# The order of VectorE's products in a head's preparation: near levels first, 256- and 512-token ones last

## The reference

```
S_t = diag(a_t) S_{t-1} + k_t v_t^T ;  o_t = S_t^T q_t
score(t, s) = sum_d q[t,d] k[s,d] exp(b[t,d] - b[s,d]),  s <= t,  b = cumsum(log a)
o_t = sum_s score(t, s) v_s
```

## Time and profile before

| | |
|---|---|
| median of 3 runs | 1294.83 us (1294.48 to 1295.87) |
| the profiled execution | 1293.82 us |
| its span in the trace | 1292.1 us |
| TensorE busy | 1235.5 us, 96% of the span |
| VectorE busy | 599.9 us, 46% |
| ScalarE busy | 415.4 us, 32% |
| GpSimd busy | 85.2 us, 7% |
| mean granted TensorE clock | 0.988 of 2.4 GHz |

### The profile page before, as it was taken

One profiled execution on the slowest core, in us unless ns is written; L12 is line 12 of the kernel. 1 busy time (PEld: TensorE's weight loads), 2 busy tenths in 40 slices (PEclk: granted clock), 3 DMA queues, 4 the chain that ended last, 5 costly groups with the idle time before them and its releaser, 6 DMA issues.

```text
span 1292.1 us, 15169 instructions
## 1 busy us (share of the span) xinstructions
PE 1235.5 (96%) x6099; PEld 1021.0 (79%) x6099; DVE 599.9 (46%) x714; ACT 415.4 (32%) x442; POOL 85.2 (7%) x121
## 2 busy tenths in 40 slices
PE   4699999999999999989999999999999999999996
PEld 3578888888889997867887788888988888888885
DVE  6855556456343667456645333335523233232221
ACT  4522322222222365343434322223422222222222
POOL 5100000000000032022310000000000000000000
PEclk9999999999999999988999999999999999999998
DMA  9276555555252422111221222243123332222311
GB/s 379 66 241 193 172 171 178 195 184 165 90 184 93 131 65 66 35 39 60 66 66 33 66 83 85 93 130 98 48 83 97 97 97 97 97 89 67 114 57 65
DMA packets 119789, 143.40 MB, mean 111 GB/s; under 512 B 3892, under 2 KB 102336, under 8 KB 119744
## 3 DMA queue, kind: packets, MB, share of 16 engines
q1 hardware_dynamic: 119560, 142.69, 33.6%
q10 hardware_dynamic: 184, 0.07, 0.0%
HBM read 140.65 MB, written 2.10 MB: 110 GB/s over the span
## 4 chain that ended last, share of the span: by engine, by line
issue 48%; PE 39%; DVE 6%; ACT 3%; DMA 2%; POOL 1%; SPq 0%; ACTq 0%; POOLq 0%; DVEq 0%
PE PS L478 10%; PE PS L480 10%; PE PS L479 10%; PE PS L682 3%; DVE ACC L1300 2%; PE PS L608 1%; ACT WH L873 1%; PE PS L521 1%; DMA RAW<-in_w_in_mix_dram 1%; PE PS L522 1%; PE PS L523 1%; DMA RAW<-in_ffn_w_in_dram 1%; DVE W L1440 1%; PE PS L722 1%; DVE WL L1200 0%
## 5 line engine op out<-in xcount | busy, mean ns | idle before, releaser
L478 PE MATMUL PS<-HH,WH 128*128 128x512 f32 (+1 forms) x1064 | 416.9, 392 | 7.4 <-DVE HL L1222 4.0
L479 PE MATMUL PS<-HL,WH 128*128 128x512 f32 (+1 forms) x1064 | 408.1, 384 | 0.0
L480 PE MATMUL PS<-HH,WL 128*128 128x512 f32 (+1 forms) x1064 | 408.0, 383 | 0.0
L1200 DVE TENSOR_TENSOR WL<-RAW,WH 128x2048 fp32r<-128x2048 f32 (+1 forms) x97 | 216.9, 2236 | 345.1 <-ACT WH L873 345.1
L873 ACT ACTIVATE WH<-RAW 128x2048 fp32r<-128x2048 f32 (+1 forms) x97 | 180.8, 1864 | 407.8 <-PE PS L480 370.6
L478 PEld LDWEIGHTS PS<-HH,WH 128*128 128x128 f32 x1064 | 201.2, 189 | 53.1 <-issue 6.8
L480 PEld LDWEIGHTS PS<-HH,WL 128*128 128x128 f32 x1064 | 201.1, 189 | 43.2
L479 PEld LDWEIGHTS PS<-HL,WH 128*128 128x128 f32 x1064 | 201.4, 189 | 41.3 <-issue 1.1
L478 PE MATMUL PS<-UH,WH 128*128 128x512 f32 (+1 forms) x372 | 140.2, 377 | 0.0
L479 PE MATMUL PS<-UL,WH 128*128 128x512 f32 (+1 forms) x372 | 139.8, 376 | 0.0
L480 PE MATMUL PS<-UH,WL 128*128 128x512 f32 (+1 forms) x372 | 139.6, 375 | 0.0
(11 more groups left out here) (225 smaller groups left out, 1187.6 us busy)
## 6 DMA issues: line engine op xcount, KB each, us to landing
RAW<-in_ffn_w_in_dram SPq DMA_DIRECT2D x44, 1024.0 KB, 5.2
ADAW<-in_w_ada_dram SPq DMA_DIRECT2D x56, 512.0 KB, 5.6
RAW<-in_w_in_mix_dram SPq DMA_DIRECT2D x22, 1024.0 KB, 5.2
RAW<-in_ffn_w_down_dram SPq DMA_DIRECT2D x16, 1024.0 KB, 5.2
ADA<-in_w_ada_dram SPq DMA_DIRECT2D x8, 1024.0 KB, 14.0
RAW<-in_ffn_w_down_dram SPq DMA_DIRECT2D x7, 768.0 KB, 4.8
RAW<-in_w_out_dram SPq DMA_DIRECT2D x3, 1024.0 KB, 5.1
XST<-in_x_dram SPq DMA_DIRECT2D x4, 512.0 KB, 5.1
```

Of the source, the lines that this page charges most:

```text
L478: mm(ps, whi, ahi, start=start, stop=False)
L479: mm(ps, whi, alo, start=False, stop=False)
L480: return mm(ps, wlo, ahi, start=False, stop=stop)
L1200: V.tensor_tensor(WL[s][:, 0:size], RAW[s][:, 0:size], WH[s][:, 0:size].bitcast(F32), ALU.subtract)\
```

## The change

The block of `decayed` that forms W256 and W512 moves behind the loop over the near levels; its instructions are the same. As the order of the 18 increments of `prep` is changed with it, TensorE's near batches now wait for 6, 10 and 14 of a preparation's increments (before: 10, 14 and 18), and the far scores for all 18 (before: 6).

```
-                pe.wait_ge(prep, 18 * p + 6 + 4 * (g + 1))
+                pe.wait_ge(prep, 18 * p + 2 + 4 * (g + 1))
...
-                pe.wait_ge(prep, 18 * p + 6)
+                pe.wait_ge(prep, 18 * p + 18)
...
                 V.tensor_tensor(KL[:, :], KL[:, :], k, ALU.mult).then_inc(prep, 1)
-                dve.wait_ge(exps, 10 * p + 3)
-                dve.wait_ge(prep, 18 * p + 2)
-                (W256: four products, W512: two products)
                 for l, B in enumerate(LEVELS):
                     h = B // 2
                     dve.wait_ge(exps, 10 * p + 4)
                     qp = QP[:, l, :].rearrange("p (n h) -> p n h", h=h)
                     V.tensor_tensor(qp, qp, blocks(q, B)[:, :, h:B], ALU.mult).then_inc(prep, 1)
                     dve.wait_ge(exps, 10 * p + 5 + l)
                     kp = blocks(KP[:, l, :], B)[:, :, 0:h]
                     V.tensor_tensor(kp, kp, blocks(k, B)[:, :, 0:h], ALU.mult).then_inc(prep, 1)
+                dve.wait_ge(exps, 10 * p + 3)
+                dve.wait_ge(prep, 18 * p + 2)
+                for src, c0 in ((KL, 0), (QU, 2)):
+                    for j in range(2):
+                        cs = slice(4 * j + c0, 4 * j + c0 + 2)
+                        ins = V.tensor_tensor(blocks(W256[:, :], CHUNK)[:, cs, :], blocks(src[:, :], CHUNK)[:, cs, :],
+                                              FT[:, 0, cs].unsqueeze(2).to_broadcast([P, 2, CHUNK]), ALU.mult)
+                    ins.then_inc(prep, 1)
+                for src, c0 in ((KL, 0), (QU, 4)):
+                    cs = slice(c0, c0 + 4)
+                    V.tensor_tensor(blocks(W512[:, :], CHUNK)[:, cs, :], blocks(src[:, :], CHUNK)[:, cs, :],
+                                    FT[:, 1, cs].unsqueeze(2).to_broadcast([P, 4, CHUNK]), ALU.mult).then_inc(prep, 1)
```

More of the change, by code:

```diff
@@ L1433, in decayed @@
                 V.tensor_tensor(KL[:, :], KL[:, :], k, ALU.mult).then_inc(prep, 1)
+                for l, B in enumerate(LEVELS):
+                    h = B // 2
+                    dve.wait_ge(exps, 10 * p + 4)
+                    qp = QP[:, l, :].rearrange("p (n h) -> p n h", h=h)
+                    V.tensor_tensor(qp, qp, blocks(q, B)[:, :, h:B], ALU.mult).then_inc(prep, 1)
+                    dve.wait_ge(exps, 10 * p + 5 + l)
+                    kp = blocks(KP[:, l, :], B)[:, :, 0:h]
+                    V.tensor_tensor(kp, kp, blocks(k, B)[:, :, 0:h], ALU.mult).then_inc(prep, 1)
                 dve.wait_ge(exps, 10 * p + 3)
@@ L1447, in decayed @@
                                     FT[:, 1, cs].unsqueeze(2).to_broadcast([P, 4, CHUNK]), ALU.mult).then_inc(prep, 1)
[L1448 to L1455, removed]
             diag = SC[:, :].rearrange("p (i x) -> p i x", x=5 * P)[:, :, 0:P]
```

## The result

The changed kernel takes 1282.3 us (median of 4 runs, 1280.62 to 1284.87) against 1295.35 us before (4 runs, 1294.48 to 1296.1). The ratio is 0.9906, 95% interval 0.9887 to 0.9925, so it is faster by 13 us. The forecast was 1280.5 with a range of 1278.7 to 1287.0. The profiled execution took 1284.87 us, the slowest of the four; its span is 1283.1 us.

The account below looks back on a forecast made before the run. TensorE, with work for 96% of the span, was taken as the bound. Waits 5.2 plus clock 9.7, less 0.1 and 0.5 of new waits, gave 14.3 us gained: 1280.5 us, range 1278.7 to 1287.0.

Parts of the forecast that it names:

- The waits: First near scores of heads 1 to 3: waits shrink to 1.04, 1.42 and 1.15 us, 5.2 us gained in sum.
- the plain price: Head 3: near products at 0.75 us beside GpSimd throughout, scores at 593.12; the forecast took 592.95, GpSimd finishing earlier.
- The clock: Low-clock stretches behind the waits of heads 1 to 3 mostly vanish: 9.7 us gained, ends 0 and 9.9.
- unit 10: Next weights in head 3: TensorE arrives before their split is ready, a new wait of 0.5 us.
- the first rival: Clock still falls in one or more heads, 1.7 to 3.3 us per fall: 1282.2 to 1287 us; 30%.
- the second one's milder form: Clock falls in all three heads, each low stretch half as long: 1284.8 us; 11% for the whole rival.
- the case that it was worked out for: Forecast case: shortened waits in heads 1 to 3 and clock mostly up there, 1280.5 us, spanning 1279 to 1282; 50%.
- stays up: Clock mostly at full behind the remaining waits of 1.0 to 1.4 us in heads 1 to 3; forecast case 50%.
- one row of a 0.95 us wait: Evidence for the clock term: 0.95 us of standing before the L553 sums leaves the clock at full.
- What comes late: VectorE leaves head 0's step 0.85 us late, 0.1 us new wait; 0.5 us new wait for head 3's next weights.
- Head 1's copies: Mask copies done by 519.95, third near batch would come at 520.6: just no wait.
- The third and fourth rivals: Third: waits not shortened, 1294.8 us, 5%. Fourth: slower, VectorE stands for QP exponentials, 1298.2 us at worst, 4%.

Follow-up runs that it names:

- the two half changes: New order only in preparations of heads 1 to 3: 1283.85 us; only in head 0 and both GLA pairs: 1293.58 us; kernel before beside both 1293.04 us.
- filling alone: Kernel before, old order, with 11, 12 and 11 unread matmuls in the waits of heads 1 to 3: 1283.39 us against 1293.04.
- the three sets: The changed kernel measured three times against the kernel before: 1282.3 us against 1295.35, 1282.68 against 1294.16, 1281.49 against 1293.1.
- the five profiles with these waits: Changed kernel three times (1282.3, 1282.68, 1281.49 us), new order in heads 1 to 3 alone (1283.85), only levels 64 and 32 before the wide products (1283.99).
- the complement: New order only in the preparations of head 0 and of the two GLA pairs, against the kernel before: 1293.58 us against 1293.04, ratio 1.0007.
- the filled kernel: Changed kernel with 4, 5 and 5 unread matmuls in the remaining waits of heads 1 to 3, second set: 1281.49 us, changed kernel beside it 1281.49.
- two levels first: Against the changed kernel, only near products of levels 64 and 32 stand before the wide products, the other eight behind: 1283.99 us, ratio 0.9916 to kernel before.
- the first two that make levels 64 and 32 first: Changed kernel with these levels made first on GpSimd, ScalarE and VectorE: 1281.93 us; also wide products behind the weight split, before the mask copies: 1282.0 us.

## Why the prediction was right, step by step

*The waits.* Forecast 1.04, 1.42 and 1.15 us, measured 0.96, 1.34 and 1.25; gained 5.3 us where 5.2 were said. The price of 0.75 us for a near product beside GpSimd, taken from two rows of head 0, held in each head (0.70 to 0.76). In head 3 the estimate that GpSimd ends before the fourth product was wrong by 0.1 us: the expectation by the plain price, 1.32, was on the other side. The restriction to heads 1 to 3 was shown by the two half changes.

*The clock.* This is the term that was mis-sized. I put it at 9.7 us, with the clock staying up. That the low clock behind the old waits costs that much was right (9.65 us by filling alone, 9.2 in its trace). But after the change it still falls in most profiled passages, 3.4 us each. By the section: 10.66 us gained in all, less 5.3 of waits, plus the 0.4 at unit 10 and some 0.3 of small waits, leaves 6.1 us for the clock. The same sum on the medians of the three sets (13.05, 11.5 and 11.6 us gained) leaves 8.4, 6.9 and 7.0. What happened is the first rival (the clock still falls in one or more heads, 1282.2 to 1287), and in two other profiles the second one's milder form (in all three heads, half as long). The range was made to reach there, and the medians of 1282.3, 1282.7 and 1281.5 lie in it. That they lie within 2.2 us of 1280.5 doesn't bear out the case that it was worked out for: none of the five profiles with these waits has the clock up in all three heads. I gave "stays up" 50% on one row of a 0.95 us wait; that wait stood between matmuls of 256 columns, not ahead of thin ones. The rule weighed there (the Trainium skill, TensorE: Matmul & The Clock Gate, Part 1: how busy TensorE has recently been sets its clock) was the better guide than that row: 11 falls of 15 behind the short waits agree with it. The falls with TensorE busy throughout (0.57 over 12.00 us of work) agree with it only if thin matmuls count as little work, which no run here isolates.

*What comes late.* Head 0: 2.60 us of standing as forecast. Counted from the start of QU, VectorE leaves the step 0.62 us late where I had 0.85, and the third batch comes 3.24 us after the second where before it was 3.17: the 0.1 us that was forecast. Unit 10: 0.41 us for a forecast of 0.5. In heads 1 to 3 I had VectorE leave each step 0.1 to 0.3 us earlier; it leaves at the same time (within 0.01 us), since what the W products save goes to the near products that now stand beside GpSimd. Head 1's copies: "just no wait" was 0.15 us short (that batch comes 4.73 us after the second, where before it was 4.57). What I had left out there is that GpSimd is slowed too: its six KP differences take 5.09 us for 4.57, ScalarE's work behind them ends 0.5 us later, and VectorE stands 0.35 us for head 0's output before it gets to the copies.

*The rest.* The whole came to 13.05 us by the medians, where 14.3 were forecast. The third and fourth rivals did not occur.

## What to carry to other kernels

Ahead of a wait on the bounding engine, look at what the releasing engine does that this wait doesn't need; moving it behind cost 0.1 us here, because its later reader had over 7 us of room. A wait in front of thin matmuls can be worth twice its length, as the clock falls with it, here 3.1 us for each 3 us of standing; dummy matmuls in the wait show this share in one experiment. When the wait goes, follow the bounding engine to its next gates before counting the gain: 3.6 us of waits came back whole until the mask copies and the weight split had been moved ahead in VectorE's list.

## What the runs showed of the hardware that was not expected

- The clock falls with TensorE busy all the time: in head 6 before and after (granted clock 0.83 over 10 us), and for over 10 us in head 4 of the filled kernel (0.57 over 12 us) and of three other kernels (two levels first, and the first two that make levels 64 and 32 first: 0.61 over 13 us).
- The low stretches come in the lengths 3.4, 6.8 and about 10 us, and behind the same work and wait they differ: head 1 has 6.8 us before and 3.4 us in the complement, both behind 2.87 us. Runs of one kernel differ too, 17 of the kernel before on one chip lie between 1289.09 and 1298.47 us; how much of that is the clock isn't shown.
- VectorE beside GpSimd pays per instruction more than per element: from start to start a W product of 128 columns takes 0.62 us (the first of the four 0.44) and one of 256 columns 0.75, alone 0.20 and 0.34. So where GpSimd works, few large instructions are what one wants there.
